# Reordering the chunk of a chunked linear recurrence on four engines, inside a two-layer trunk kernel

## The reference

```python
def step(s, inp):
    r_t, w_t, k_t, v_t, a_t, b_t = inp
    sa = jnp.einsum('bhvk,bhk->bhv', s, a_t)
    s = s * w_t[:, :, None, :] + sa[..., None] * b_t[:, :, None, :] + v_t[..., None] * k_t[:, :, None, :]
    y = jnp.einsum('bhvk,bhk->bhv', s, r_t) if emit else None
    return s, y
...
for d, reverse in enumerate((False, True)):
    s_ctx, y_c = rwkv_scan(s0, r_c, w_c, k_c, v_c, -kk_c, kk_c * a_c, reverse, need_ctx)
    _, y_l = rwkv_scan(s_ctx, r_l, w_l, k_l, v_l, -kk_l, kk_l * a_l, reverse, True)
```

## Time and profile before

| | |
|---|---|
| median of 3 runs | 2920.68 us (2918.13 to 2920.90) |
| the profiled execution | 2914.61 us |
| its span | 2912.7 us |
| TensorE, VectorE, ScalarE, GpSimd busy | 95%, 41%, 22%, 2% |
| layer 0's recurrence, from the first key rates | 139.0 to 356.0 us |
| layer 1's recurrence | 1409.9 to 1628.6 us |

### The profile page before, as it was taken

One profiled execution on the slowest core, in us unless ns is written; L12 is line 12 of the kernel. 1 busy time (PEld: TensorE's weight loads), 2 busy tenths in 40 slices (PEclk: granted clock), 3 DMA queues, 4 the chain that ended last, 5 costly groups with the idle time before them and its releaser, 6 DMA issues.

```text
span 2912.7 us, 59776 instructions
## 1 busy us (share of the span) xinstructions
PE 2776.7 (95%) x26982; PEld 1666.4 (57%) x26982; DVE 1200.8 (41%) x2544; ACT 655.4 (22%) x1361; POOL 59.9 (2%) x55
## 2 busy tenths in 40 slices
PE   8988899999999999999878999989999999999997
PEld 4467767445777888864567787863333333333332
DVE  4777665445646444246777564431011010111101
ACT  2334312444322111012443126620000000000000
POOL 0011000000000000000020000000000000000000
PEclk9999999999999999999999999989999999999999
DMA  7100134112232433232000442459999999999995
GB/s 291 58 3 3 36 137 141 56 53 73 101 123 80 145 116 89 80 120 83 30 3 3 150 163 91 149 195 348 416 361 366 413 360 383 396 364 413 363 379 202
DMA packets 188773, 534.30 MB, mean 183 GB/s; under 512 B 6113, under 2 KB 80097, under 8 KB 171105
## 3 DMA queue, kind: packets, MB, share of 16 engines
q1 hardware_dynamic: 187440, 526.21, 48.1%
q0 software_dynamic: 1072, 4.19, 0.4%
HBM read 528.29 MB, written 2.10 MB: 182 GB/s over the span
## 4 chain that ended last, share of the span: by engine, by line
PE 89%; DVE 6%; ACT 3%; issue 1%; DMA 1%; SPq 0%; DVEq 0%; ACTq 0%
PE bank L584 66%; PE bank L712 12%; PE bank L1353 8%; ACT WR L1643 2%; PE bank L1215 1%; DVE WR L2450 1%; PE bank L830 1%; DMA WR<-in_low_first 1%; ACT ar L1643 0%; DVE ar L2395 0%; DVE HT L2416 0%; DVE ar L2419 0%; DVE WR L2445 0%; DVE WR L2454 0%; DVE ar L2488 0%
## 5 line engine op out<-in xcount | busy, mean ns | idle before, releaser
L584 PE MATMUL bank<-AT,WR 128*128 128x512 f32 (+1 forms) x1408 | 519.9, 519 | 4.9 <-ACT AT L1643 3.7
L1643 ACT ACTIVATE ar<-bank 128x256 f32<-128x256 f32 (+2 forms) x338 | 155.1, 463 | 1533.1 <-PE bank L584 1026.1
L584 PE MATMUL bank<-WR,ar 128*32 128x512 f32 (+1 forms) x4464 | 444.5, 555 | 1.6 <-DVE ar L2912 1.6
L584 PE MATMUL bank<-ar 128*32 128x512 f32 (+6 forms) x3990 | 429.6, 509 | 9.6 <-ACT ar L1643 5.7
L584 PEld LDWEIGHTS bank<-AT,WR 128*128 128x128 f32 x1408 | 262.2, 191 | 211.1 <-issue 196.3
L584 PEld LDWEIGHTS bank<-ar 128*32 128x32 f32 (+3 forms) x3990 | 176.1, 124 | 248.3 <-issue 237.1
L584 PEld LDWEIGHTS bank<-WR,ar 128*32 128x32 f32 x4464 | 143.7, 110 | 288.4 <-issue 285.8
L584 PE MATMUL bank<-AT,ar 128*32 128x512 f32 (+1 forms) x1456 | 151.6, 562 | 12.3 <-ACT AT L1643 12.3
L2922 DVE TENSOR_TENSOR YB<-YB,bank 128x512 f32<-128x512 f32 x28 | 18.0, 684 | 343.3 <-PE bank L584 343.3
L2930 DVE TENSOR_TENSOR ar<-ar,bank 128x512 f32<-128x512 f32 (+1 forms) x48 | 29.8, 621 | 286.5 <-PE bank L584 285.1
L1643 ACT ACT_TABLE_LOAD x111 | 142.4, 1283 | 15.5 <-DVE ar L2308 7.8
(11 more groups left out here) (371 smaller groups left out, 3355.2 us busy)
## 6 DMA issues: line engine op xcount, KB each, us to landing
WR<-in_moe_w_down SPq DMA_DIRECT2D x27, 2048.0 KB, 14.4
WR<-in_ada_w SPq DMA_DIRECT2D x20, 2048.0 KB, 8.5
ar<-in_moe_w_down SPq DMA_DIRECT2D x20, 2048.0 KB, 14.6
WR<-in_w_in SPq DMA_DIRECT2D x18, 2048.0 KB, 9.5
WR<-in_moe_w_gate SPq DMA_DIRECT2D x18, 2048.0 KB, 16.6
WR<-in_moe_w_up SPq DMA_DIRECT2D x15, 2048.0 KB, 16.1
WR<-in_moe_w_up SPq DMA_DIRECT2D x18, 1536.0 KB, 7.7
WR<-in_moe_w_gate SPq DMA_DIRECT2D x15, 1536.0 KB, 8.9
```

The source lines that it names most:

```text
L584: return pe.matmul(o, lhsT, rhs, start=first, stop=last)
L1643: return act.activation(out, in_, func, **k)
```

## The change

It writes the chunk in another order on all engines. On TensorE the level 0 product of the next chunk comes right behind G, the turned inverse becomes a step of its own (`inverse_turned`) behind it, the solution follows the next chunk's first growth, y and the state move one step later each, the turned values are interleaved with level 2's second product and the against pairs move one place later. For this level banks, grown bank, gram bank and right side get fixed banks, T1 gets two buffers, the turned inverse a buffer per parity, and the matrix LT only one. On VectorE the wait for G goes, the operands are split in two, and state, predicated copy and transpositions change places. ScalarE forms the key rates of both directions in four operations instead of eight, at another place. Centring of chunk i+2 moves from VectorE to GpSimd. The number of TensorE products stays.

```diff
-        def level_banks(i, n):
-            return [banks[6 * (i % 2)], banks[1]]
...
-        solved_bank, gram_bank = banks[2], banks[7]
+                    [x2[:, 512 * n:512 * n + 512] for n in (1, 0)], [x2[:, 512 * n:512 * n + 512] for n in (3, 2, 6)] + [HTf[:, 3584:4096]],
+                    [x2[:, 512 * n:512 * n + 512] for n in (4, 7)], x2[:, 2560:3072])
+
+        level_banks, grown_bank, gram_bank, right_bank = banks[0:2], banks[6], banks[7], banks[2]
+
+        def turned_inverse(XT, i, n):
+            return XT[(1, 3)[i % 2] if n else 0]
...
+        def centre_of(engine, i):
+
+            rows = Rc.rearrange("p d j c w -> p d j (c w)")
+            middle = by_direction(rows, i, CW, 32, 1)
+            return engine.tensor_tensor(CC.rearrange("p (d j) w -> p d j w", d=2), by_direction(rows, i, CW, 0, CW),
+                                        middle.to_broadcast([128, 2, 4, CW]), ALU.subtract)
...
-                        if i:
-                            pe.wait_ge(A.free, A.jobs[("G", l, i - 1)])
...
+                def inverse_doubled(i, n, values=False):
+                    x, t1 = turned_inverse(XT, i, n), T1[i % 2]
...
+                    if values and i:
+                        pe.wait_ge(A.free, A.jobs[("U", l, i - 1, 1)])
...
+                        for h in range(2 if values else 0):
+                            value_turned(i, q, h)
+
+                def inverse_turned(i):
+                    x, t1 = turned_inverse(XT, i, 4), T1[i % 2]
+                    pe.wait_ge(turned_ready, seen(turned_ready))
+                    pe.wait_ge(S.free, S.jobs[("T1", l, i, 4, 1)])
+                    for q, h in hq:
+                        last = mm(pair(gram_bank, q, 1 - h), pair(t1, q, 1 - h), pair(x, q, 1 - h), True, True)
...
                 for i in range(NCH):
                     if i:
-                        level(i, 0)
-                        pe.wait_ge(A.free, A.jobs[("XT", l, i - 1, 4)])
-                        for q, h in hq:
-                            solve(i - 1, q, h)
+                        inverse_turned(i - 1)
                         inverse_doubled(i, 0)
+                        solve(i - 1)
+                        level(i, 1)
+                        inverse_doubled(i, 1)
                         y_of_chunk(i - 1, ybank)
-                        level(i, 1)
-                        state(i - 1)
-                        inverse_doubled(i, 1)
                         if i <= 4:
                             bonus(i - 1)
-                        level(i, 2, "values")
+                        level(i, 2)
+                        state(i - 1)
+                        inverse_doubled(i, 2, values=True)
                         pe.wait_ge(responses_ready, seen(responses_ready))
                         against(i, 0)
-                        inverse_doubled(i, 2)
-                        against(i, 2)
                     level(i, 3, "X" if i < NCH - 1 else None)
+                    against(i, 2)
+                    inverse_doubled(i, 3)
                     against(i, 4)
-                    inverse_doubled(i, 3)
+                    level(i, 4, "LT" if i < NCH - 1 else None)
                     against(i, 6)
-                    level(i, 4, "LT" if i < NCH - 1 else None)
                     if i == 0:
                         pe.wait_ge(uv_cleared, seen(uv_cleared))
                     ybank = from_state(i)
-                    inverse_doubled(i, 4)
-                pe.wait_ge(A.free, A.jobs[("XT", l, NCH - 1, 4)])
-                for q, h in hq:
-                    solve(NCH - 1, q, h)
+                    from_values(i)
+                    if i < NCH - 1:
+                        level(i + 1, 0)
+                inverse_turned(NCH - 1)
+                solve(NCH - 1)
                 y_of_chunk(NCH - 1, ybank)
...
+            def rates(l, i):
+
+                if i:
+                    act.wait_ge(operands_ready, 8 * l + i)
...
+                for j in range(4):
+                    x = Ra[:, 0, j, CH * i:CH * i + CH]
+                    both = bass.AP(x.tensor, x.offset, [list(p), [d[0] + CH * (BWD[i] - i), 2], [1, CH]])
+                    f(key_rate[:, :, j, :], both, ACT.Identity, scale=V(l, "k_a", j), bias=cv1[:, j:j + 1])
...
-                for j in range(4):
-                    f(key_rate[:, d, j, :], Ra[:, d, j, CH * c:CH * c + CH], ACT.Identity, scale=V(l, "k_a", j),
-                      bias=cv1[:, j:j + 1])
...
+                rates(l, 1)
                 for d in range(2):
                     decays(l, 1, d)
                 for i in range(NCH):
-                    for n in range(5):
+                    for n in range(4):
                         if n == 0 and i:
-                            stacked_in(slice(0, 64), solved_bank, 1)
+                            copied(G, right_bank)
+                            copied(XT[2], gram_bank)
+                        copied(X[1], grown_bank)
+                        if n == 0 and i:
+                            stacked_in(slice(0, 64))
+                        if n == 1 and i + 2 < NCH:
+                            rates(l, i + 2)
                         if n == 2:
-                            stacked_in(slice(64, 128), gram_bank, 1)
...
+                            stacked_in(slice(64, 128))
                         if n in (2, 3) and i + 2 < NCH:
                             decays(l, i + 2, n - 2)
...
                     if i:
                         masked(i, 0)
                         if i < NCH - 1:
-                            dve.wait_ge(A.full, A.jobs[("G", l, i - 1)])
                             rates_in(l, i + 1)
                         turned(i, 0)
                         if i < NCH - 1:
-                            operands(l, i + 1)
+                            updates(l, i + 1)
                         masked(i, 1)
+                        if i < NCH - 1:
+                            operands_scaled(l, i + 1)
+                            responses(l, i + 1)
+                        turned(i, 1)
                         if not (l == 1 and i - 1 < 4):
                             emitted(i - 1)
-                        if i < NCH - 1:
-                            responses(l, i + 1)
-                        turned(i, 1)
-                        state(i - 1)
                         if i <= 4:
                             bonus_out(i - 1)
                     masked(i, 2)
...
+                    else:
+                        state(i - 1)
+                    turned(i, 2)
                     kept(i, 0, 2)
-                    turned(i, 2)
-                    if i + 2 < NCH:
-                        centre(l, i + 2)
-                    kept(i, 2, 4)
                     masked(i, 3)
-                    kept(i, 4, 6)
-                    turned(i, 3)
                     if i < NCH - 1:
                         begin_inverse(i + 1)
-                    kept(i, 6, 8)
+                    kept(i, 2, 4)
+                    turned(i, 3)
+                    kept(i, 4, 5)
                     masked(i, 4)
+                    kept(i, 5, 8)
                     if i < NCH - 1:
                         begin_turned(i + 1)
...
                     if i < 4:
                         bonus(l, i)
+                    if i + 2 < NCH:
+                        pool.wait_ge(responses_ready, 8 * l + i + 2)
+                        centre_of(pool, i + 2).then_inc(centred, 1)
```

More of the change, by code:

```diff
@@ L264, in trunk @@
         MV = HTf[:, 0:3072].rearrange("p (b n w) -> p b n w", b=2, n=3)
-        LTs = [HTf[:, 3072 + 512 * b:3584 + 512 * b] for b in range(2)]
+        LT = HTf[:, 3072:3584]
         CC = ar[:, TR0 + 8 * 512:TR0 + 8 * 512 + 8 * CW].rearrange("p (q w) -> p q w", q=8)
@@ L856, in value_turned @@
                     c = CH * (i if q < 4 else BWD[i])
[L857 removed]
+                    last = mm(pair(right_bank, q, 1 - h), Rv[64 * h:64 * h + 64, q % 4, c:c + CH],
                               eye[64 * h:64 * h + 64, 64 * h:64 * h + 64], True, True)
@@ L861, in value_turned, with solve @@
                         A.done(("vt", l, i, h))
-                def solve(i, q, h):
-                    last = mm(pair(solved_bank, q, 1 - h), pair(XT[2], q, 1 - h), pair(G, q, 1 - h), True, True)
-                    if q == 7:
-                        last.then_inc(A.full, 1)
-                        A.done(("U", l, i, h))
+                def solve(i):
+                    pe.wait_ge(A.free, A.jobs[("XT", l, i)])
+                    for q, h in hq:
+                        last = mm(pair(right_bank, q, 1 - h), pair(XT[2], q, 1 - h), pair(G, q, 1 - h), True, True)
+                        if q == 7:
+                            last.then_inc(A.full, 1)
+                            A.done(("U", l, i, h))
                 def gram(i, what, bank, q, h):
@@ L917, in inverse_doubled @@
                         for h in range(2):
-                            if n < 4:
```

(32 more changed lines are left out.)

82 lines of the change are left out of this document (31 added, 51 removed).

## The result

| | before | changed |
|---|---|---|
| median | 2919.95 us (2918.13 to 2920.90, 4 runs) | 2869.72 us (2869.00 to 2870.51, 4 runs) |
| profiled execution | 2914.61 us | 2869.00 us |
| its span | 2912.7 us | 2867.2 us |
| again, on another chip | 2917.57 us (2912.61 to 2918.70, 9 runs) | 2872.22 us (2870.19 to 2875.09, 5 runs) |

The change is faster by 1.5 to 1.7%: ratio 0.9829 [0.9812, 0.9846], on the other chip 0.985 [0.9836, 0.9863]. Forecast were 2876 and 2866 to 2893. The medians differ by 50.2 us on the first chip and by 45.4 on the other, the profiled spans by 45.5; the sum of the prediction was made against the profiled execution and gave 44.9.

The account below looks back on a forecast made before the run. Each recurrence was taken as bound by a chain across engines, none full. Terms -15.9 (layer 0), -19.7 (layer 1), -2.3 (key rates), -6 (stalls), -1 (clock) gave -44.9: 2876 us on the median's scale, range 2866 to 2893.

Parts of the forecast that it names:

- the walk: Recurrence chunk summed interval by interval from trace durations: plain chunk 20.03 us against 23.42 measured, good to 0.3 us.
- the clock term: TensorE's 1.2 GHz stretches behind the idle ahead of each recurrence: -1 us taken, bounds nothing to -4.7.
- The 1.29 idle goes: TensorE's idle before level 4 vanishes: predicated copy precedes the last transposition, decays are 1.29 long instead of 2.62.
- Bonus chunk: Chunks 1 to 3: 23.06 us each, with 1.06 for the bonus product and 1.97 for level 3's late copy.
- its worst case: VectorE and GpSimd excluding each other for 1.3 us in all 12 chunks with moved centring: 16 us of gain lost.
- By layer: The two recurrences without stalls: layer 0 -15.9 us (tail +1.4), layer 1 -19.7 us.
- Key rates: ScalarE's eight operations become four at 0.38 apart, shortening the wait ahead of each recurrence: -2.3 us for both layers.
- Stalls: TensorE's issue waits in the recurrences, read as late instruction loads, shrink by spreading dense products: -6 of 6.9 us.
- A: Rival: stalls in the recurrences move, loads being late elsewhere as often; gain 38.9, 2882 us; chance 0.2.
- B: Rival: the walk is too smooth, TensorE blocks cost 10% more; gain 28, 2893 us; chance 0.12.
- C: Rival: centring on GpSimd takes far longer than 1.27 us, delaying level 3's copy; at 8 us, 2935; chance 0.03.
- D: Rival: the time is given back behind the recurrence by a late weight stream; 2920 us; chance 0.03.

Follow-up runs that it names:

- e7: Changed kernel with VectorE's predicated copy of the next gram back behind the last transposition: 2895.28 us, ratio 0.9926 to the kernel before.
- e3: Kernel before with only ScalarE's eight key-rate operations made four of twice the columns, behind the second direction's exponentials: 2913.22 us, ratio 0.9994.
- e1: Changed kernel with GpSimd centring chunk i+2 ahead of the four bonus operations instead of behind them: 2867.34 us, ratio 0.9833 to the kernel before.
- e6: Changed kernel with centring ahead of the bonus, as in e1, measured beside e5: 2869.38 us, ratio 0.9835 to the kernel before.
- e2: Changed kernel with centring done twice on GpSimd: 2881.03 us (one run).
- e4: Kernel before with 128 more TensorE instructions (repeated gram products) once, ahead of chunk 0 of layer 0: 2915.47 us (one run).
- e10 to e12: Changed kernel with 64, 128 and 192 more TensorE instructions ahead of chunk 0 of layer 0: 2879.21, 2872.87 and 2877.02 us (one run each).
- e8: Changed kernel with the last pair of against products back ahead of level 4: 2893.86 us, ratio 0.9919 to the kernel before.
- e9: Changed kernel with the solution back ahead of the next chunk's first growth, ScalarE stacking it ahead of that growth's copy: 2899.84 us (one run).
- e5: Changed kernel unaltered, as yardstick of a later session on another chip: 2872.22 us, ratio 0.9850 to the kernel before.

## Why the prediction was right

The mechanism held: idle time of the chain went, where the walk said, and the stalls went. The sum came out closer than its terms deserve: the split of layer 0 was off by 3 us at chunk 0 and by as much the other way in the bonus chunks, and the clock term was wrong.

- **Plain chunk**, forecast 20.03, measured 20.43. The intervals were 3.78, 3.97, 4.26, 4.20 and 3.82; they came out at 4.00, 4.10, 4.23, 4.31 and 3.79. Level 1 to 2 was off most (0.22): TensorE's growth begins 1.83 behind the level product, and growth and y then take 1.08 and 1.09. Level 2 to 3 was mis-sized because I ended it with ScalarE's copy; TensorE's growth with the values (1.10) and the against pair (0.85) in front of level 3 end later. The walk over the old order had been good to 0.3, this one was good to 0.4.
- **Level 3 to 4.** "The 1.29 idle goes": it did, and e7 shows by what, the place of the predicated copy. e3 shows that the shorter ScalarE queue, which I named beside it, gives nothing alone.
- **Bonus chunk**, forecast 23.06, measured 22.03, 22.39 and 22.50 in layer 0. The step that failed is the 1.97 of level 3's copy. Level 3 to 4 took 4.63, 5.16 and 5.10, so 0.4 to 0.9 more than in the plain chunk (in layer 1 0.6 to 1.0), and in the second of them by a wait of 0.94 for VectorE's kept products, not for ScalarE. Centring took 1.07, not 1.27, and the against pair in front of level 4 covers part of the copy's delay, which I had charged whole. e1 and e6 remove the cost and gain about 2 us per layer (1.6 to 2.9); e2 raises it.
- **Two engines on SBUF.** The scaling of the state (L2495) took 0.70 beside the bonus in layer 0 and 0.86 in layer 1, where it takes 0.15 or 0.16 without, for the 0.65 priced, and in the second and third bonus chunk one GpSimd operation took 1.61 to 1.73 for 1.27. All 12 centrings on GpSimd took 1.07, also the one at 239.54 beside VectorE's predicated copy and kept products, which read PSUM. The Trainium skill's exclusive lock (SBUF — State Buffer, "SBUF: two separate sides") agrees with the scaling at 234.75: it ends at 235.45, just behind the GpSimd operation that began at 234.15 and took 1.28. It cost 0.55 to 0.7 us there, and nothing in centring: its worst case did not come.
- **By layer.** Forecast -15.9 and -19.7 without stalls. Measured -18.6 and -23.9 with 2.9 and 3.7 of issue waits in them, so -15.7 and -20.2. Layer 0's agreement is partly luck. The level 3 products of chunks 1 and 4, in the kernel before and in the changed one:

```profile
196.38 0.27 PE L584 MATMUL bank<-WR,HT 64*64 64x64 f32 x2
274.07 0.27 PE L584 MATMUL bank<-WR,HT 64*64 64x64 f32 x2
```

```profile
192.89 0.27 PE L591 MATMUL bank<-WR,HT 64*64 64x64 f32 x2
259.81 0.27 PE L591 MATMUL bank<-WR,HT 64*64 64x64 f32 x2
```

From the first predicated copy (146.12 and 143.91) to the first of them the change gains 1.3 for the 4.4 forecast. From there to the second it gains 10.8, 7.5 without the issue waits, for the 4.0 forecast. The plain chunks gave 8.2 for 8.9, again without the issue wait, and the tail cost 1.3 for 1.4. Chunk 0 gives little because TensorE now waits 1.88 in it for VectorE's mask of level 2, where the old order had an against pair and 0.48 of wait, and 1.20 for the kept products:

```profile
169.52 0.27 PE L591 MATMUL bank<-WR 64*64 64x64 f32 x2 [1.88 <-DVE WR L2460]
```

- **Key rates.** 1.63 for four, 0.41 each (forecast 0.38 apart); VectorE's waits 2.25 in both layers for the 2.2 forecast: -2.2 for the -2.3. By these waits the term holds; in the whole time no run resolves it (e3).
- **Stalls.** Forecast -6 of 6.9, measured -6.6. e4 and e10 to e12 fit the reading as instruction loads: positions of one phase in 256 in every kernel, and at most 1.5 us at the four phases of the new order. The Trainium skill (Runtime: NRT & Kernel Launch, "Instruction fetch mechanics") holds such loads to be hidden, with branches the exception; these waits of 0.2 to 1.7 us stand between plain products, so if they are loads, the trace doesn't agree. The cause stays open as far as no run shows a load arriving late. That the new order helps because it issues more slowly at the boundaries is consistent with all this, but the one run made to undo it (e8) failed to.
- **Clock**, forecast -1, and wrong: nothing. With the wait shortened from 4.81 to 3.71 the granted clock behind it was at 1.2 GHz for as long as before (3.4 and 6.8 us); it varies from profile to profile in either order (in layer 0 it is 6.8 in e3 and e4, and none in e9). What I had not asked is what the new waits do. Behind the 1.88 in chunk 0 the clock stayed at 2.4 GHz in the first profile of the changed kernel, but in e5, the same kernel, it was at 1.2 GHz for 3.4 us in layer 1 (the wait is at 1424.79):

```profile
1426.20:1429.60 3.40, 3.40 (x74) 2.84 (x72) 2.51 (x6) 2.78 (x8) 0.00 (x0) 0.50 0.02 5
```

Nine of the eleven profiles in the new order (its variants included) have such a stretch there in one layer or both, the three in the old order none. No run prices it by itself.

- **The scale.** I added 6.1 for the distance between the profiled execution and the median of before. The changed kernel's medians lie 0.7 from its own profiled execution. That accounts for most of the 6 us between 2876 and 2870, and it is no part of the mechanism.

Rivals A (2882) and B (2893) are both excluded by the traces: the stalls are all but gone, and the plain chunk came within 0.4 of the walk. C fell with centring's 1.07, D with the last stretch of the table, +0.1.

## What to carry to other kernels

Where no engine is full, walk the chain interval by interval with durations from the trace, and check the walk on the old order first; then look at each in-order queue for the instruction that a late operand holds up in front of a ready one: moving one 0.69 us copy ahead of a transposition that waits was worth half of this change in e7, though such shares don't add up. Charge a late result only with what TensorE has no other product to cover. And look at a shared ring of banks before moving a product earlier: it can arrive and find no bank.

## What the runs showed of the hardware that I had not expected

- A longer wait of TensorE can cost about twice what is added to it. In e2 a wait that grew from 0.78 to 1.93 was followed by 3.4 us at 1.2 GHz, which lost another 1.2; behind the 0.78 the clock had stayed at 2.4 GHz. The wait's length alone doesn't decide it: behind the 1.88 of chunk 0 the same kernel had either.
- TensorE's waits without a releaser in the recurrences, 0.2 to 1.7 us long, stand in the thirteen profiles that have them at 193 to 195 modulo 256 of its records, in kernels of quite different order. I read them as late instruction loads; that is argued, not shown. Adding 128 instructions ahead moved all of them, so a few microseconds (1.7 more in layer 0 and 3.0 less in layer 1 with the old order) can come from code that has nothing to do with the place that stalls.
